# Another opening for a streaming hybrid step: half vectors feature-major, first norm from input rows, transfers in the first product's order

## The reference, cut to what matters

```python
ada = (jax.nn.silu(c) @ w_ada + b_ada).reshape(B, N_MOD, D_MODEL)
xn = _modulate(_rms(x, g_ffn1), ada[:, 0], ada[:, 1])
x = x + 0.5 * ada[:, 2][:, None] * _swiglu(xn, w_ffn1_gate, w_ffn1_up, w_ffn1_down)
xn = _modulate(_rms(x, g_mix), ada[:, 3], ada[:, 4])
m, new_buf, h_last, v_state = _mixer(xn, ...)      # projections of 6 x 1024 columns, RG-LRU, spatial gating, w_out
x = x + ada[:, 5][:, None] * m
xn = _modulate(_rms(x, g_ffn2), ada[:, 6], ada[:, 7])
x = x + 0.5 * ada[:, 8][:, None] * _swiglu(xn, w_ffn2_gate, w_ffn2_up, w_ffn2_down)
...
def _modulate(xn, shift, scale):
    return xn * (1.0 + scale[:, None, :]) + shift[:, None, :]
def _swiglu(x, w_gate, w_up, w_down):                 # hidden width 2816
    return (jax.nn.silu(x @ w_gate) * (x @ w_up)) @ w_down
```

## Time and profile before

| | |
|---|---|
| median of 3 runs | 2510.47 us (2510.26 to 2513.07) |
| the profiled execution | 2516.07 us, of which its span is 2514.3 us |
| TensorE (PE) busy | 2411.8 us, 96% of the span, 11469 matmul records |
| VectorE (DVE) | 1672.5 us, 67% |
| ScalarE (ACT) | 1053.6 us, 42% |
| GpSimd (POOL) | 148.2 us, 6% |
| mean granted TensorE clock | 0.982 of full |

### The profile page before, as it was taken

The page is one execution under the profiler, slowest core; times in us unless marked ns, Lnnn a source line. Parts: engine busy times, 40 slices in busy tenths (PEclk is TensorE's granted clock), DMA queues, the critical chain, the costliest instruction groups (busy, mean ns, idle before and its releaser), DMA issues.

```text
span 2514.3 us, 31914 instructions
## 1 busy us (share of the span) xinstructions
PE 2411.8 (96%) x11469; PEld 2030.0 (81%) x11469; DVE 1672.5 (67%) x2660; ACT 1053.6 (42%) x1825; POOL 148.2 (6%) x186
## 2 busy tenths in 40 slices
PE   7889999999999999999999999988999999999997
PEld 3567777777788877999999999986777788878886
DVE  4976767766666685666666666469677667656666
ACT  3454444444333353433344434135444444433334
POOL 3000000000000000000111110000000000000000
PEclk9999999999999999999999999989999999999998
DMA  9244554455976333312222123413544543497642
GB/s 359 72 159 151 176 176 150 151 177 184 346 263 226 134 126 104 127 54 63 63 63 61 56 59 98 152 55 117 175 149 151 174 147 123 151 353 278 226 134 78
DMA packets 245521, 381.03 MB, mean 152 GB/s; under 512 B 16658, under 2 KB 158154, under 8 KB 243991
## 3 DMA queue, kind: packets, MB, share of 16 engines
q1 hardware_dynamic: 232702, 345.15, 39.6%
q0 software_dynamic: 10240, 33.56, 4.9%
q10 hardware_dynamic: 2456, 0.75, 0.1%
HBM read 262.93 MB, written 116.47 MB: 151 GB/s over the span
## 4 chain that ended last, share of the span: by engine, by line
PE 71%; DVE 15%; DMA 5%; issue 4%; ACT 3%; SPq 1%; DVEq 0%; ACTq 0%
PE bank L512 21%; PE bank L513 20%; PE bank L514 20%; DMA h_dram<-stage_lo 3%; DVE u_lo L604 3%; PE bank L2800 2%; PE bank L2802 2%; PE bank L2803 2%; DMA wraw<-in_w_ffn_down 1%; DVE stage_lo L1932 1%; DVE wraw L631 1%; DVE ada_lo L1947 1%; PE bank L2818 1%; DVE h L1940 1%; DVE x L2110 1%
## 5 line engine op out<-in xcount | busy, mean ns | idle before, releaser
L604 DVE TENSOR_TENSOR u_lo<-wraw,u_hi 128x512 fp32r<-128x512 f32 (+2 forms) x532 | 317.4, 618 | 285.6 <-ACT u_hi L598 282.8
L512 PE MATMUL bank<-ops,u_hi 128*128 128x512 f32 x1232 | 488.5, 397 | 13.5 <-ACT g L1201 10.5
L513 PE MATMUL bank<-ops,u_hi 128*128 128x512 f32 x1232 | 485.3, 394 | 0.0
L514 PE MATMUL bank<-ops,u_lo 128*128 128x512 f32 x1232 | 484.2, 393 | 0.0
L598 ACT ACTIVATE u_hi<-wraw 128x512 fp32r<-128x512 f32 (+2 forms) x532 | 289.2, 567 | 267.3 <-PE bank L514 167.6
L512 PE MATMUL bank<-xn_hi,w_hi 128*128 128x384 f32 x1104 | 370.1, 335 | 6.2 <-ACT ww L1606 2.0
L514 PE MATMUL bank<-xn_hi,w_lo 128*128 128x384 f32 x1104 | 368.8, 334 | 0.0
L513 PE MATMUL bank<-xn_lo,w_hi 128*128 128x384 f32 x1104 | 368.8, 334 | 0.0
L512 PEld LDWEIGHTS bank<-ops,u_hi 128*128 128x128 f32 x1232 | 234.3, 190 | 77.4 <-ACT g L1201 11.3
L514 PEld LDWEIGHTS bank<-ops,u_lo 128*128 128x128 f32 x1232 | 233.8, 190 | 50.8
L513 PEld LDWEIGHTS bank<-ops,u_hi 128*128 128x128 f32 x1232 | 234.4, 190 | 49.1
(11 more groups left out here) (321 smaller groups left out, 4257.3 us busy)
## 6 DMA issues: line engine op xcount, KB each, us to landing
h_dram<-stage_hi SPq DMA_DIRECT2D x154, 256.0 KB, 2.4
h_dram<-stage_lo SPq DMA_DIRECT2D x154, 256.0 KB, 2.7
ada_raw<-in_w_ada POOLq DMA_DIRECT2D x96, 256.0 KB, 3.0
raw<-in_w_in SPq DMA_DIRECT2D x48, 512.0 KB, 4.7
wraw<-in_w_ffn_gate SPq DMA_DIRECT2D x44, 512.0 KB, 3.9
wraw<-in_w_ffn_up SPq DMA_DIRECT2D x44, 512.0 KB, 4.9
wraw<-in_w_ffn_down SPq DMA_DIRECT2D x48, 384.0 KB, 4.7
x<-x_dram SPq DMA_DIRECT2D x6, 2304.0 KB, 12.0
```

What stands on the lines that cost most here:

```text
L512: nc.tensor.matmul(out, hi, mov_hi, start=first, stop=False, skip_group_check=True)
L513: nc.tensor.matmul(out, hi, mov_lo, start=False, stop=False, skip_group_check=True)
L514: return nc.tensor.matmul(out, lo, mov_hi, start=False, stop=last, skip_group_check=True)
L604: nc.vector.tensor_tensor(unit(u_lo, f, g, u, n), unit_source(u, n), unit(u_hi, f, g, u, n).bitcast(F32), ALU.subtract).then_inc(u_lo_read ...
```

## The change: what it does, and its diff

- The six half vectors are computed feature-major: 32 matmuls for each, with a 128x128 block of w_ada as the weights and the nine columns of silu(c) moving. ScalarE's row copies and TensorE's turns of them go. Their order becomes SCALE1 and SHIFT1 first halves, then the second halves, then GATE1. Halves 0 and 1 stay ahead of the first product; halves 2 to 5 go into the first round, around the first sample matmuls, behind S2 and behind S3.
- The first norm's squares are summed by ScalarE along the rows of the input tiles (row_squares, with an accumulated output), and its factors are made as those of the later norms: root, reciprocal and spread of a few columns, factor_copy. GpSimd's additions and the matmuls with ones for this norm go.
- SP's queue issues six row tiles, halves 0 and 1 and two weight pieces, a spill, the last row tiles, halves 2 and 3, two weight pieces, a spill, the relay store, a spill, half 4, a spill, half 5. The last three row tiles are turned behind the first product.
- The first block's samples are made in two halves of four tiles in a buffer of their own (first_samples, first_samples_shifted, first_samples_lo); their multiply, scale, shift and low part are the operations of samples_modulated and sample_operand at half the size.
- The copies of S3's results (snap_up 4 and 5) move ahead of units 14 and 15's high parts and the first Silu, and O_B22's high parts ahead of O_T4's.
- In the second block reciprocal(2, 1) moves ahead of the last two tiles of O_B21's low parts, spread(2, 1) between the K tiles of the second product, the samples' high and low parts ahead of the scaling, and units 10 and 11 ahead of O_T1's low parts (in the first block too).
- The output product's first pair takes token third by token third and releases each bank on its own.

The diff, cut to its core:

```diff
-FIRST_HALVES = [(v, half) for v in (SCALE1, SHIFT1, GATE1) for half in range(2)]
+FIRST_HALVES = [(SCALE1, 0), (SHIFT1, 0), (SCALE1, 1), (SHIFT1, 1), (GATE1, 0), (GATE1, 1)]
+FIRST_BANKS = (7, 6, 7, 2, 7, 7)
...
-            sp.wait_ge(x_loaded[1], 16)
+            def spill(rows, stored, cols=slice(0, TOK)):
+                sp.dma_start(x_dram[:, rows, cols], x[:, rows, cols]).then_inc(stored, 16)
             ada_half(0)
             ada_half(1)
-            first_weights(0)
+            weights(0, 0, 0, 0)
+            weights(0, 0, 1, 0)
+            sp.wait_ge(x_in, 8)
+            spill(slice(0, KH), x_spilled, slice(0, PH))
+            tile_rows(sp, 2)
             ada_half(2)
             ada_half(3)
-            def spill(rows, stored):
-                sp.dma_start(x_dram[:, rows, :], x[:, rows, :]).then_inc(stored, 16)
-            sp.wait_ge(x_in, 2 * NT)
-            spill(slice(0, KH), x_spilled)
-            spill(slice(KH, KT), x_spilled_late)
-            ada_half(4)
+            weights(0, 0, 0, 1)
+            weights(0, 0, 1, 1)
+            sp.wait_ge(x_spilled, 16)
+            spill(slice(KH, KT), x_spilled, slice(0, PH))
             sp.wait_ge(rg_loaded, 64)
             sp.dma_start(rg_dram.rearrange("k p n -> p k n"),
                          rg_sb[:, :, :, :].rearrange("p k g n -> p k (g n)")).then_inc(rg_stored, 16)
+            sp.wait_ge(x_in, 2 * NT)
+            spill(slice(0, KH), x_spilled_late, slice(PH, TOK))
+            sp.wait_ge(sumsq_mm, 9)
+            ada_half(4)
+            sp.wait_ge(x_spilled_late, 16)
+            spill(slice(KH, KT), x_spilled_late, slice(PH, TOK))
             sp.wait_ge(rg_stored, 16)
             ada_half(5)
             ffn(0)
...
+            def row_squares(lo, hi):
+                for t in range(lo, hi):
+                    act.wait_ge(x_loaded[t // 3], 32 if t >= 6 else 16)
+                    if t > 1:
+                        act.wait_ge(sumsq_mm, t - 1)
+                    nc.scalar.activation(spent[:, t % 2, :], xrow[:, t, :], ACT.Square, accum_out=nrst[:, t:t + 1])\
+                      .then_inc(sumsq_mm, 1)
...
+                if f == 0 and o in (O_B11, O_B21):
+                    act.wait_ge(ada_ready, 2 if o == O_B11 else 4)
+                elif f == 0 and o == O_T3:
                     act.wait_ge(ada_mm, 5)
                 elif f == 0 and o == O_T4:
                     act.wait_ge(ada_mm, 6)
...
-                    if g == 0:
-                        snap_up(g, 4, E_P7[0], g22[:, :], bank[XB[0]][:, :])
-                        snap_up(g, 5, E_P7[1], h22[:, :], bank[XB[1]][:, :])
...
                         op_hi(f, O_B11)
-                        op_hi(f, O_B21)
-                    samples_hi(f)
-                    if f == 0:
-                        first_rows(4)
-                    begin(0)
-                    begin_up(0)
-                    if f == 0:
-                        first_rows(5)
+                        row_squares(6, NT)
+                        root(0, 1)
+                        root(0, 2)
+                        begin(0)
+                        begin_up(0)
+                        factor_copy(0, 1)
+                        factor_copy(0, 2)
+                        samples_hi(f, 0)
+                        for u in range(4, 8):
+                            unit_hi(act, f, 0, u)
+                    else:
+                        begin(0)
+                        begin_up(0)
                     unit_hi(act, f, 0, 8)
                     unit_hi(act, f, 0, 9)
-                    op_hi(f, O_T1)
+                    if f == 0:
+                        op_hi(f, O_B21)
+                        samples_hi(f, 1)
                     unit_hi(act, f, 0, 10)
                     unit_hi(act, f, 0, 11)
+                    op_hi(f, O_T1)
                     op_hi(f, O_T2)
                     op_hi(f, O_T3)
                     unit_hi(act, f, 0, 12)
...
                     act.wait_ge(op_lo_ready, 28 * f + 20)
                     snap_up(0, 2, E_P6[0], g12[:, :], bank[XB[0]][:, :])
                     snap_up(0, 3, E_P6[1], h12[:, :], bank[XB[1]][:, :])
+                    op_hi(f, O_B22)
                     op_hi(f, O_T4)
-                    op_hi(f, O_B22)
+                    snap_up(0, 4, E_P7[0], g22[:, :], bank[XB[0]][:, :])
+                    snap_up(0, 5, E_P7[1], h22[:, :], bank[XB[1]][:, :])
...
+            row_squares(0, 6)
+            act.wait_ge(sp_step, 1)
+            nc.scalar.activation(spw[:, 1, :], spw[:, 0, :], ACT.Exp, scale=-1.0).then_inc(sp_exp, 1)
+            root(0, 0)
...
+                dve.wait_ge(samples_act, FACTORS_MADE[i, c])
+                if f == 0:
+                    dve.wait_ge(mod_step, 1 if kk < KH else 2)
+                    dve.wait_ge(*((x_spilled, x_spilled_late)[c], 16 if kk < KH else 32))
...
+                if f == 1:
+                    for k in range(KH):
+                        op_scale(f, k, 1)
...
                 def first_round():
 
                     if f == 0:
+                        x_turned_in(2)
+                        reciprocal(0, 1)
+                        reciprocal(0, 2)
+                        first_samples(0)
+                        first_samples_shifted(0)
+                        first_samples_lo(0)
+                        for i in range(1, 5):
+                            weight_sum(dve, 0, 0, i)
+                        unit_lo(dve, 0, 0, 4)
+                        unit_lo(dve, 0, 0, 5)
+                        weight_sum(dve, 0, 0, 5)
+                        weight_sum(dve, 0, 0, 6)
+                        unit_lo(dve, 0, 0, 6)
+                        unit_lo(dve, 0, 0, 7)
+                        first_half(2)
+                        dve.wait_ge(ada_ready, 3)
+                        scale_gain(SCALE1, KH, KT)
                         for k in range(KH):
                             op_scale(f, k + KH, 0)
+                        first_samples(1)
+                        for k in range(KH):
+                            op_scale(f, k, 1)
+                        unit_lo(dve, f, 0, 8)
+                        unit_lo(dve, f, 0, 9)
+                        first_half(3)
+                        dve.wait_ge(ada_ready, 4)
+                        shift_difference(0)
                         op_lo(f, O_B21)
-                    sample_operand(f)
+                        first_samples_shifted(1)
+                        first_samples_lo(1)
+                    else:
+                        sample_operand(f)
                     for k in range(KH):
                         op_sum_(f, O_T1, k)
-                    if f == 0:
-                        first_half(4)
-                        first_half(5)
-                    unit_lo(dve, f, 0, 8)
-                    unit_lo(dve, f, 0, 9)
+                    if f == 1:
+                        unit_lo(dve, f, 0, 8)
+                        unit_lo(dve, f, 0, 9)
                     for k in range(KH):
                         op_scale(f, k + KH, 1)
-                    op_lo(f, O_T1)
                     unit_lo(dve, f, 0, 10)
                     unit_lo(dve, f, 0, 11)
+                    op_lo(f, O_T1)
                     for k in range(KH):
                         op_sum_(f, O_T2, k)
                     weight_sum(dve, f, 0, 7)
                     op_lo(f, O_T2)
                     for k in range(KH):
                         op_sum_(f, O_T3, k)
+                    if f == 0:
+                        first_half(4)
                     op_lo(f, O_T3)
                     unit_lo(dve, f, 0, 12)
                     unit_lo(dve, f, 0, 13)
                         op_sum_(f, O_T4, k)
                     op_lo(f, O_T4)
                     op_lo(f, O_B22)
+                    if f == 0:
+                        first_half(5)
                     unit_lo(dve, f, 0, 14)
                     unit_lo(dve, f, 0, 15)
...
-            dve.wait_ge(x_in, 2 * NT)
             dve.wait_ge(sp_step, steps[0])
+            dve.wait_ge(x_in, 12)
+            reciprocal(0, 0)
             first_half(0)
+            dve.wait_ge(ada_ready, 1)
+            scale_gain(SCALE1, 0, KH)
+            for u in range(4):
+                unit_lo(dve, 0, 0, u)
+            for k in range(KH):
+                op_scale(0, k, 0)
             first_half(1)
-            dve.wait_ge(ada_ready, 2)
-            scale_gain(SCALE1)
-            reciprocal(0, 0)
-            first_half(2)
-            reciprocal(0, 1)
-            first_half(3)
-            dve.wait_ge(ada_ready, 4)
-            shift_difference(0)
-            reciprocal(0, 2)
-            first_units(0)
-            dve.wait_ge(mod_step, 2)
-            dve.wait_ge(x_spilled, 16)
-            first_operand(0)
-            dve.wait_ge(x_spilled_late, 16)
+            op_lo(0, O_B11)
...
             samples_modulated(2, xs, xs, xs)
+            reciprocal(2, 1)
             op_lo(1, O_B21, slice(2, 4))
-            reciprocal(2, 1)
```

(55 more changed lines are left out.)

265 lines of the change are left out of this document (106 added, 159 removed).

## The result

The changed kernel takes 2528.53 us in the median (2528.0 to 2536.62, 5 runs), against 2510.47 before: 1.0076 times as long, 95% interval 1.0065 to 1.0088. Its profiled execution took 2528.39 us, 2526.6 of it span, so the two profiled executions lie only 12.3 us apart where the medians lie 18.1 apart: that of before was 5.6 above its median, this one is at its own.

A forecast was written before the change was run, and what follows sets the result against it. TensorE holds 71% of the chain, though VectorE bounds the first round. First gated h +27, moved copies -1, second FFN's opening -7, output product -0.9 sum to +18 us: median 2510.47 to 2528.5, range 2515 to 2541.

The forecast's parts named there:

- the case: Total time of the changed kernel: slower than before, chance 0.76, against same 0.07 and faster 0.17.
- The clock: TensorE's granted clock falls to about 0.50 in the first round's half vectors, adding 29.4 us at the first gated h.
- the term for recovery: Products behind halves regain the clock slowly: +2 behind the first product, +2.2 behind the third and the fifth half.
- the softplus term: Opening: VectorE's softplus chain takes 11.5 us after the Exp, ends at 31.9 and bounds the first product, at 41.9.
- The steps before the fifth half: First round: first product 41.9, turns, spreads, third and fourth halves, products to 95.6 at full clock, before the clock's additions.
- The half at full clock: Each half vector's 64 records on TensorE take 7.3 us, between 6.8 and 7.9.
- The full-clock schedule: Opening and first round at TensorE's full clock: first product at 41.9, first gated h at 129.9 against 132.25 before.
- The waits for T3's and T4's memory: First round: high parts wait for the fifth and sixth halves, leaving VectorE idle 10 and 10.7 us at its adds.
- 11 us of handovers: First round: 11 us of the first product's 42.8 us lead goes to handovers behind the halves.
- The moved copies: First round: S3's result copies move ahead of the Silu, ScalarE makes B22 before T4; counted at -1.0 us.
- The second block: Second FFN's opening: earlier low part and spread let VectorE have its unit sooner, -7 us, bounds -4.4 and -7.1.
- The output product's: Output product: finished banks released one by one, so the 0.91 us wait goes, -0.9 us.

The follow-up runs named there:

- 117 columns: Changed kernel with the nine moving columns of each half vector's matmul repeated 13 times, copies not read: 2505.11 us, ratio 0.9972.
- moving two calls: Kernel with nine columns repeated to 117, fifth half vector moved ahead of S1 and sixth behind S2: 2494.01 us, ratio 0.993.
- the run with the old opening: Kernel with nine columns repeated to 117, the second feed-forward block's opening back in the order of before: 2512.8 us, ratio 1.0004.
- T4 first: Changed kernel with O_T4's high parts ahead of O_B22's again in the second block alone: 2528.18 us, ratio 1.0062.
- with 36: Changed kernel with the nine moving columns repeated four times, to 36: 2528.61 us, ratio 1.0071.
- the third move: Kernel with 117 columns and fifth half ahead of S1, with the sixth half ahead of S2 too: 2500.49 us, ratio 0.9947.

## Why the prediction was right, and where its steps were not

The total (2528 forecast, 2528.53 measured), the sign and the case were right, and the chain of events runs as it was laid out: the halves start at full clock and fall to 0.50, T3's and T4's high parts wait for them, and the lead of the first product becomes a lag at the first gated h. That the median was met to 0.1 us is luck. The profiled execution was forecast at 2534 and took 2528.39, since the lag at h was 21.1 us and not 27; and the 5.6 us by which the profiled execution of before lay above its median, which the forecast took off, were scatter too. One term was mis-sized and some small ones were wrong.

- *The clock* was forecast at 29.4 us on the first gated h. 117 columns took back 25.4 there and 23.4 of the total. The halves took 12.3, 13.7, 10.4, 11.4, 11.2 and 10.2 us, against 14.0 forecast for the second and 11.2 for the later ones. What failed in part is the term for recovery, 2 us behind the first product and 2.2 each behind the third and the fifth half. Against 117 columns it is 1.8, 1.7 and nothing: the products behind the fifth half are as slow with 117 columns, behind the same wait of 3.90 us. And 2.3 us of the fourth half's cost are covered by a wait for VectorE. The other way, the first product pays 10.3 instead of 7.4, by the softplus term below.
- *The steps before the fifth half* ran 4.4 us ahead of mine (110.56 against 115.0): the first product 1.3, mostly since the first half ran its first 1.7 us at full clock and was not slow throughout, the turns and spreads 0.5, the third half 0.8, what follows it 0.5, and the handover behind the fourth half, taken as 3.4 us where TensorE waited 1.92, 1.5 (the fourth half itself gives 0.2 back). At the first h it is 5.9 (153.37 against 159.3), of which 1.0 is the sixth half.
- *The half at full clock*, taken as 7.3 us between 6.8 and 7.9 of the nearest rows, took 7.29 to 7.31 with 117 columns. Nine columns never ran a whole half at full clock.
- *The full-clock schedule* gave h at 129.9; with 117 columns it came at 127.92. Here a step failed: "the softplus chain ... runs on VectorE for 11.5 us, so the chain ends at 31.9". It took 4.5 us and ended at 24.0, because GpSimd's additions, which the change removes, were what had stretched it. With the slow clock the first half ended at 31.67, behind the chain either way, so this error hid; at full clock it made the first product 37.7 instead of 41.9, and h 2.0 earlier. That it did not matter for the total is luck too: it needed the slow first half.
- *The waits for T3's and T4's memory* came as forecast: 13.77 and 15.48 us of VectorE's idle time, 3.90 and 2.76 of TensorE's. The second stands before T4's low parts and not before the sixth add, which comes later (149.34) and waits for nothing. That they are a cost of their own, of 8 to 10 us, was in the sum (11 us of handovers) but not named as avoidable; moving two calls avoids it.
- *The moved copies* were counted at -1.0 in the first block and nothing in the second. Measured as a whole: nothing. Between the two kernels the first block's stretch from h to the first piece's matmuls shrank from 29.3 to 27.2 us, but the copies account for 0.7 of these 2.1; what the rest is stays open. B22 before T4, which I had counted at nothing, adds VectorE's wait of 2.54 in the second block, and the late store, which no step of mine had, takes more back in the first.
- *The second block* was counted at -7, bounds -4.4 and -7.1. The step that it rests on, units 8 and 9, came 8.0 us sooner; at the first gated h 5.5 of them were left (55.17 us behind the sample sums before, 49.71 after), since the wait for T4's high parts lies between. By the run with the old opening the part is worth 5.4 at h and 8.0 in the totals, with an uncertainty of 4 there; -7 holds, the second digit does not.
- *The output product's* wait of 0.91 us is gone from the trace; by itself it was not tried.

The sum of the terms as the traces show them does not close the gap between 12.3 and 18.1. In the profiled pair the lag is 21.1 us at the first h, 19.0 at the first piece's matmuls (161.57 and 180.58), 22.2 at the sample sums, 16.7 at the second block's first h, and 12.1 near the end. The rise by 3 in the middle is the late store, in the changed kernel the one at 374.77, 4.35 us long, with TensorE's wait of 2.36 us and the slow products behind it (the lag is 18.9 at 231.82 and 21.9 at 433.48). All runs with the copies moved have it; why that order of the copies makes one store, 200 us later, late stays open. The fall from 16.7 to 12.1 lies where both kernels do the same work, the moved copies apart: two stores of h take 3.90 and 4.53 us in the kernel before and 2.44 and 3.18 in the changed one.

```profile
1749.21 3.90 DMA h_dram<-stage_lo
...
1950.62 4.53 DMA h_dram<-stage_lo
```

```profile
1765.80 2.44 DMA h_dram<-stage_lo
...
1965.74 3.18 DMA h_dram<-stage_lo
```

From the second block's first h to the end the fourteen traces take between 780.8 and 789.2 us, these two 786.7 and 782.3. Most of the 5.8 us between 12.3 and 18.1 is thus scatter of single executions, and so is some of the lag at the first h: two executions with the same opening, that of the changed kernel and that with T4 first, had their first h at 153.37 and 148.02, with the halves' clock at 0.50 to 0.69 and at 0.50 to 0.83. The second took 2520.8 us, 7.4 below its own median. So a single pair of traces gives the clock's cost at h as 25.4, another as 18 to 20; the medians' 23.4 carry the conclusion, and the split by steps is that of one pair.

## What to carry to other kernels

A matmul that is cheap by its columns can be dear by the clock at which it runs. In the traces shown here a half took 8.5 to 13.7 us with nine moving columns and 7.30 with 117 (from the third half on), and a record with 117 columns (0.114 us) cost hardly more than one with a single column at full clock (0.106); so more moving columns, read again and thrown away, were the cheaper form. Price such work at both clock levels before moving it. A lead won at the first product is worth only what reaches the end of the stage; follow it to the event from which both kernels do the same work. And where operands lie over the weights of a small product, do that product before they are due: moving two calls gave 10.5 us. It ends where TensorE's own work is the bound; the third move gave nothing.

## What the runs showed of the hardware that I had not expected

- *The same records ran at full clock with more columns.* 64 records back to back, TensorE busy all the time: 0.50 to 0.83 with 9 columns and with 36, 1.00 with 117 from the third half on. The Trainium skill ("TensorE: Matmul & The Clock Gate", Part 1) ties the clock to how busy TensorE is; by the profile's busy time, 11.18 of 11.18 us at 0.62 against 7.30 of 7.30 at 1.00, busy alone does not tell the two apart.
- *GpSimd stretches small VectorE steps.* A 128x8 TENSOR_SCALAR took 1.17 us beside GpSimd's 128x512 additions (9.71 us for seven) and 0.17 without them; the 128x8 TENSOR_TENSOR steps between took 0.17 in both. The Trainium skill ("SBUF — State Buffer", section "SBUF: two separate sides") says that VectorE and GpSimd take a shared pair of ports as an exclusive lock; by that rule a step waits out the addition that is under way, and for the TENSOR_SCALAR steps the trace agrees: 1.17 and the short step come to about the 1.39 us of one addition. That section of the Trainium skill counts VectorE operations with two SBUF inputs in as well; the TENSOR_TENSOR steps have two and were not stretched. All but the first began right behind a stretched step, so they may have fallen between two additions, which no run separates.
